# The forget row moved into the low keys' free rows: two score products a step in the second block's attention

## What is computed

```python
def forgetting_attention(q, k, v, log_f):
    """q, k, v: (B, H, S, Dh); log_f: (B, H, S) float32 log forget gates."""
    c = jnp.cumsum(log_f, axis=-1)
    qf = q.astype(jnp.float32) * (Dh ** -0.5)
    for i in range(S // Q_BLOCK):
        q0, q1 = i * Q_BLOCK, (i + 1) * Q_BLOCK
        logits = jnp.einsum('bhqd,bhkd->bhqk', qf[:, :, q0:q1], kf[:, :, :q1])
        logits = logits + c[:, :, q0:q1, None] - c[:, :, None, :q1]
        logits = jnp.where(s_pos <= t_pos, logits, -jnp.inf)
        p = jax.nn.softmax(logits, axis=-1)
        outs.append(jnp.einsum('bhqk,bhkd->bhqd', p, vf[:, :, :q1]))
```

## Time and profile of the kernel before

| | us |
|---|---|
| three runs | 1095.19, 1095.08, 1096.62 |
| median | 1095.19 |
| the profiled execution, its own time | 1095.96 |
| its span in the profile | 1094.1 |
| around the span | 1.9 |
| mean granted clock of TensorE, share of full speed | 0.997 |
| busy TensorE matmuls, share of the span | 97% |
| busy VectorE | 81% |
| busy ScalarE | 61% |
| busy GpSimd | 17% |

### The profile page before, as it was taken

The page is one execution under the profiler, slowest core; times in us unless marked ns, Lnnn a source line. Parts: engine busy times, 40 slices in busy tenths (PEclk is TensorE's granted clock), DMA queues, the critical chain, the costliest instruction groups (busy, mean ns, idle before and its releaser), DMA issues.

```text
span 1094.1 us, 18024 instructions
## 1 busy us (share of the span) xinstructions
PE 1065.5 (97%) x6544; PEld 939.3 (86%) x6544; DVE 885.8 (81%) x1448; ACT 666.9 (61%) x1179; POOL 186.2 (17%) x239
## 2 busy tenths in 40 slices
PE   8999988999999999999999998999999999999997
PEld 6688876998999999888888777778899999998885
DVE  6888885798988888888684778666689889879876
ACT  7787785476555555656683477545445555566664
POOL 1486744011001111000000103300001111100000
PEclk9999999999999999999999999999999999999999
DMA  7423321766765676886536721045356676776553
GB/s 285 114 77 81 92 60 38 243 126 191 202 158 190 175 189 209 194 246 205 190 126 214 180 58 39 21 110 179 96 136 183 205 176 181 203 183 214 189 177 123
DMA packets 51320, 171.17 MB, mean 156 GB/s; under 512 B 6432, under 2 KB 7072, under 8 KB 51104
## 3 DMA queue, kind: packets, MB, share of 16 engines
q1 hardware_dynamic: 37296, 122.56, 34.3%
q0 software_dynamic: 13312, 46.14, 19.4%
q10 hardware_dynamic: 624, 1.31, 0.4%
HBM read 162.64 MB, written 48.23 MB: 193 GB/s over the span
## 4 chain that ended last, share of the span: by engine, by line
PE 84%; DVE 7%; ACT 5%; issue 2%; POOL 1%; DMA 1%; ACTq 0%; SPq 0%; DVEq 0%; POOLq 0%
PE bank L2090 11%; PE bank L2092 11%; PE bank L2091 11%; PE bank L2651 6%; PE bank L2653 6%; PE bank L2652 6%; PE bank L583 6%; PE bank L584 6%; PE bank L585 6%; PE bank L1148 2%; PE bank L1138 2%; PE bank L1093 1%; PE bank L1094 1%; PE bank L1095 1%; DVE wl L506 1%
## 5 line engine op out<-in xcount | busy, mean ns | idle before, releaser
L506 DVE TENSOR_TENSOR wl<-raw,wh 128x1024 fp32r<-128x1024 f32 (+1 forms) x144 | 169.6, 1184 | 63.1 <-ACT wh L493 61.5
L493 ACT ACTIVATE wh<-raw 128x1024 fp32r<-128x1024 f32 (+1 forms) x145 | 145.7, 1010 | 114.1 <-PE bank L2653 52.9
L2090 PE MATMUL bank<-h,wh 128*128 128x256 f32 x576 | 163.2, 283 | 2.2 <-DVE sw L2270 2.2
L2092 PE MATMUL bank<-h,wl 128*128 128x256 f32 x576 | 163.0, 283 | 0.0
L2091 PE MATMUL bank<-h,wh 128*128 128x256 f32 x576 | 163.0, 283 | 0.0
L2091 PE MATMUL bank<-hl,wh 128*128 128x256 f32 x432 | 122.3, 283 | 0.0
L2092 PE MATMUL bank<-hh,wl 128*128 128x256 f32 x432 | 122.2, 283 | 0.0
L2090 PE MATMUL bank<-hh,wh 128*128 128x256 f32 x432 | 122.2, 283 | 0.0
L2651 PE MATMUL bank<-wh,high_tokens 128*128 128x512 f32 x308 | 121.2, 394 | 0.7 <-DVE wl L506 0.7
L2653 PE MATMUL bank<-wh,low_tokens 128*128 128x512 f32 x308 | 120.0, 390 | 0.0
L2652 PE MATMUL bank<-wl,high_tokens 128*128 128x512 f32 x308 | 120.0, 390 | 0.0
(11 more groups left out here) (337 smaller groups left out, 2660.8 us busy)
## 6 DMA issues: line engine op xcount, KB each, us to landing
raw<-weights SPq DMA_DIRECT2D x163, 512.0 KB, 4.2
down_weight_sums<-weights POOLq DMA_DIRECT2D x60, 512.0 KB, 6.0
raw<-down_weight_sums SPq DMA_DIRECT2D x40, 512.0 KB, 4.0
down_weight_sums<-down_weight_sums POOLq DMA_DIRECT2D x20, 512.0 KB, 4.7
xres<-x_t SPq DMA_DIRECT2D x8, 512.0 KB, 6.7
down_weight_sums<-weights POOLq DMA_DIRECT2D x12, 256.0 KB, 4.1
sw<-ta SPq DMA_DIRECT2D x36, 64.0 KB, 2.0
raw<-down_weight_sums SPq DMA_DIRECT2D x8, 256.0 KB, 2.6
```

Source lines behind the costliest of these rows:

```text
L493: act.activation(wh[:, j, b, n], raw[:, j, b, n], ACT.Copy).then_inc(high_split, 1)
L506: v.tensor_tensor(wl[:, j, b, :], raw[:, j, b, :], wh[:, j, b, :].bitcast(F32), ALU.subtract)\
L2090: pe.matmul(o, wh_half[:, h, k, :], high[:, k, :], start=first and k == 0, stop=False, skip_group_check=True)
L2092: ins = pe.matmul(o, wl_half[:, h, k, :], high[:, k, :], start=False, stop=k == HK - 1, skip_group_check=True)
```

## The change

The forget row gets no product of its own. Its row for one head (high and low part) is put in the `other` rows of the low keys: `act_forget_rows` multiplies the 64 first rows of `cs` by the one-hot column of the head, on ScalarE, in iterations 12 to 15 of the in-projections, and `act_other_keys` goes. The second score product then takes another stationary operand, `q2[par]`: a copy of the queries' high part in `own`, ones in `other`. So it gives high queries times low keys, plus the forget row. The product of low queries with low keys is no longer computed.

`q2` has two query slots per `par`. Its ones come from one DMA per `par` on ScalarE's queue in iteration 14, its queries from one DMA per head on ScalarE's queue: the first two in iteration 16, the other six in attention steps 2, 6, 10, 14, 18 and 22, one step after the late query's high part is made. TensorE waits for the copy before a head's first score (`query_placed`).

To make room, `pr2` holds only the key blocks that are used (`ROW2`, 20 KB instead of 32 KB), and six of the eight buffers of turned probabilities move behind it; `q2` takes the place of `tb` and `sw`.

```diff
+ROW2 = [j * (j + 1) // 2 * P for j in range(QB + 1)]
...
-        pr2 = place("pr2", [P, PR2, QB, S], at=hh_at)
+        pr2 = place("pr2", [P, PR2, ROW2[QB]], at=hh_at)
...
+        pth2 = [place(f"pth2_{i}", [P, S], F32R, at=hh_at + (20 + 2 * i) * KB if i < 3 else arena + 70 * KB) for i in range(PT2)]
+        ptl2 = [place(f"ptl2_{i}", [P, S], F32R, at=hh_at + (26 + 2 * i) * KB if i < 3 else rh_at + 2 * KB) for i in range(PT2)]
+
+        q2 = [place(f"q2_{par}", [P, 2, S], F32R, at=at) for par, at in ((0, tb_at), (1, tb_at + 4 * KB))]
...
-                    if f + ph.lag[f] + 1 == m and ph.tiles[f][1] == "k":
-                        act_other_keys(act, ph, f)
+                if 12 <= m < 16:
+                    act_forget_rows(act, ph, m - 12)
+                if m == 14:
+                    act_ones_rows(act, ph)
+                if m == 16:
+                    q0 = tile_of(ph, "q", 0)
+                    act.wait_ge(ph.fin.high, ph.fin_count(q0))
+                    for par in range(2):
+                        act_place_query(act, 0, par)
...
+        def act_forget_rows(act, ph, g):
+
+            act.wait_ge(ph.fin.low, ph.low_count(IN2.index(("forget", "c", 0))))
             for par, own, other in pair():
-                ins = act.activation(ph.kl[par][other, i, :], ph.kl[par][own, i, :].bitcast(F32), ACT.Copy)
+                head = 2 * g + par
+                ins = act.activation(ph.kl[par][other, g, :], cs[0:HD, :].bitcast(F32), ACT.Copy, scale=col("onehot", head, slice(0, HD)))
             ins.then_inc(ph.keys, 1)
+
+        PLACED1 = 32 * len(PLACED)
+
+        def act_ones_rows(act, ph):
+
+            act.wait_ge(ph.fin.low, ph.low_count(ph.pools[-1]))
+            for par, own, other in pair():
+                act.dma_start(q2[par][other, :, :].rearrange("p r (b n) -> p (r b) n", n=P).bitcast(F32),
+                              ones[other, :].rearrange("p (b n) -> p b n", b=1).to_broadcast([HD, 2 * QB, P])).then_inc(f1.placed[par], 16)
+
+        def act_place_query(act, qt, par):
+
+            own = list(pair())[par][1]
+            act.wait_ge(f1.placed[par], PLACED1 + 16 * (qt + 1))
+            act.dma_start(q2[par][own, qt % 2, :].bitcast(F32), stacked[par][own, qt, :].bitcast(F32)).then_inc(f1.placed[par], 16)
+
+        def query_placed(eng, qt, par):
+
+            eng.wait_ge(f1.placed[par], PLACED1 + 16 * (qt + 2))
...
+                query_placed(pe, qt, par)
...
-            pe.matmul(o, q, in2.kl[par][:, kt, keys], start=False, stop=False)
-            pe.matmul(o, onehot[:, aux:aux + 1].to_broadcast([P, P]), cs[:, keys], start=False, stop=False)
+            pe.matmul(o, q2[par][:, qt % 2, block], in2.kl[par][:, kt, keys], start=False, stop=False)
...
+                for m, par in WAITING_HIGH:
+                    if n == WAITING_HIGH[m, par] + 1:
+                        act.wait_ge(late.high, late_count(m, par))
+                        act_place_query(act, in2.tiles[m][2], par)
```

More of the change, by code:

```diff
@@ L415, in build @@
         tq = place("tq", [P, 3, S], at=arena + 64 * KB)
-        pth2 = [place(f"pth2_{i}", [P, S], F32R, at=turn_at + 2 * i * KB if i < 3 else arena + 70 * KB) for i in range(PT2)]
-        ptl2 = [place(f"ptl2_{i}", [P, S], F32R, at=turn_at + (6 + 2 * i) * KB if i < 3 else rh_at + 2 * KB) for i in range(PT2)]
+        pth2 = [place(f"pth2_{i}", [P, S], F32R, at=hh_at + (20 + 2 * i) * KB if i < 3 else arena + 70 * KB) for i in range(PT2)]
+        ptl2 = [place(f"ptl2_{i}", [P, S], F32R, at=hh_at + (26 + 2 * i) * KB if i < 3 else rh_at + 2 * KB) for i in range(PT2)]
+        q2 = [place(f"q2_{par}", [P, 2, S], F32R, at=at) for par, at in ((0, tb_at), (1, tb_at + 4 * KB))]
         v2 = place("v2", [P, QB, 2, 4 * P], F32R, at=arena + 72 * KB)
@@ L1873, in pe_turn2 @@
             for q in range(q0, q1_):
-                ins = pe.transpose(turn_bank2(n)[:, q * P:(q + 1) * P], pr2[:, s % PR2, q, kb * P:(kb + 1) * P], ident[:, :])
+                ins = pe.transpose(turn_bank2(n)[:, q * P:(q + 1) * P], pr2[:, s % PR2, ROW2[q] + kb * P:ROW2[q] + (kb + 1) * P], ident[:, :])
             ins.then_inc(at2.turned, 1)
@@ L1906, in vec_attention2 @@
                         v.wait_ge(at2.turned, 4 * (s - PR2) + 4)
-                    v.tensor_scalar(pr2[:, s % PR2, j, lo * P:hi * P], banks[n % 3][:, lo * P:hi * P], -SCALE, None,
+                    v.tensor_scalar(pr2[:, s % PR2, ROW2[j]:ROW2[j + 1]], banks[n % 3][:, lo * P:hi * P], -SCALE, None,
                                     ALU.mult, ALU.min, accum_out=negm[:, n % 8:n % 8 + 1]).then_inc(at2.maxed, 1)
@@ L1948, in act_attention2 @@
                     act.wait_ge(at2.maxed, n + 1)
-                    p = pr2[:, s % PR2, j, lo * P:hi * P]
+                    p = pr2[:, s % PR2, ROW2[j]:ROW2[j + 1]]
                     act.activation(p, p, ACT.Exp, bias=negm[:, c], scale=-1.0, accum_out=rsum[:, c]).then_inc(at2.exped, 1)
+                for m, par in WAITING_HIGH:
+                    if n == WAITING_HIGH[m, par] + 1:
+                        act.wait_ge(late.high, late_count(m, par))
+                        act_place_query(act, in2.tiles[m][2], par)
                 for m, par in WAITING_HIGH:
@@ L1963, in gpsimd_attention2 @@
             for n in range(at2.n):
-                lo, hi = key_range("causal", n % 4)
-                p = pr2[:, (n // 4) % PR2, n % 4, lo * P:hi * P]
+                p = pr2[:, (n // 4) % PR2, ROW2[n % 4]:ROW2[n % 4 + 1]]
                 g.wait_ge(at2.inverted, n // 2 + 1)
```

3 lines of the change are left out of this document (removed).

## The result

| | before | after |
|---|---|---|
| median of 20 runs each, us | 1095.30 | 1097.49 |
| lowest to highest | 1094.76 to 1096.69 | 1095.57 to 1099.46 |
| ratio to before, 95% interval | | 1.0016 [1.0010, 1.0023] |
| the profiled execution / its span | 1095.96 / 1094.1 | 1096.74 / 1094.9 |
| granted clock of the profiled execution | 0.997 | 0.994 |

The changed kernel is slower by 0.16%. Its interval keeps this difference from zero, though it lies under the 0.2% that the prediction held for invisible. The forecast was 1096.0; 1.5 us are missing from it.

The account below looks back on a forecast made before the run. The prediction took a VectorE-ScalarE loop in the second block's attention as the bound, TensorE outside. Terms +0.8 - 0.2 + 0.2 = +0.8 us on a median of 1095.19 gave 1096.0 us, range 1092.5 to 1099.0.

Parts of the forecast that it names:

- Bound of the stage: Second block's attention, 657.0 to 697.6 us: VectorE and ScalarE form the loop, 6.09 us a head, with TensorE outside.
- Rival 1: TensorE's queue bounds the attention after all, so all 5.2 us saved there come: 1090.8 us, chance 0.12.
- The heads' pitch: First maxima of neighbouring heads in the attention stay about 6.1 us apart; falling towards 5.5 us would mean Rival 1.
- TensorE's idle time in the stage: Sign in the changed trace: TensorE's idle time in the attention goes up by about 5 us.
- Place of the forget rows: On ScalarE before the attention, all four pairs now stand behind 642 us, delaying the first maximum: +0.8 us, bounds -0.2 to +1.3.
- the splits of the output projection: On ScalarE they begin at 656.1 us instead of 654.96; VectorE starts its half at 657.2 instead of 656.40.
- scaled form: Forget rows as scaled copies on ScalarE: scale priced at nothing, bound 0.03 us each, 0.3 us in all.
- Product: Forget product removed from each score step; on the path only once, at the attention's start: 0.2 us gained, 0 to 0.6.
- Six issues: Six query-copy DMA issues on ScalarE's queue in the attention, 0.73 us each against 0.70 hidden: +0.2 us, bounds 0 to 4.4.
- Ones rows: Two DMA issues filling ones on ScalarE's queue before the attention, between third pair and split: +0 us, bound +1.5.
- First query copy: Issued by about 657.1 us at the latest, landing in 2.3 us before VectorE is ready: cost 0, bound +0.5 or more.
- The forecast end of the stage: Sign in the changed trace: the second block's attention ends at about 698.4 us, 697.6 before.

Follow-up runs that it names:

- e1: The kernel before without the forget product, so the forget row is left out of the scores: 1095.99 us, ratio 1.0000.
- e9: The kernel before without the forget product, with seven extra 128x512 matmuls on TensorE just ahead of the first score: 1095.12 us, ratio 0.9997.
- e7: The kernel before, all three products, with its eight low-key copies made by GpSimd in place of ScalarE: 1094.73 us, ratio 0.9987.
- e6: The changed kernel with the eight forget rows made by GpSimd in place of ScalarE: 1093.76 us, ratio 0.9983.
- e8: e6 with late high parts of query tiles 1 and 2 and query head 1's copies moved before the attention on ScalarE: 1093.50 us, ratio 0.9977.
- e10: The changed kernel with three extra 128x512 matmuls on TensorE ahead of its wait for the first query copy: 1096.77 us, ratio 1.0011.
- e2: The kernel before with its four pairs of key copies moved to iterations 12 to 15, where the changed kernel has forget rows: 1097.04 us, ratio 1.0011.
- e3: The changed kernel with seven extra 512-column matmuls on TensorE ahead of its wait for the first query copy: 1097.41 us, ratio 1.0017.
- e5: The changed kernel with each of the six query copies inside the attention issued as two DMAs of 32 partitions: 1099.83 us, ratio 1.0037.
- e4: The changed kernel, heads 0 and 1 using 64-row second products and a separate forget product, without waiting for query copies: 1101.33 us, ratio 1.0051.

## Why the prediction came out as it did

- **Bound of the stage** (loop of VectorE and ScalarE, TensorE outside): right. Without the product the time doesn't move (e1, e9); work taken off ScalarE moves the end of the stage by 1.25 (e7), 1.94 (e6) and 3.3 us (e8). Rival 1 is refuted. The heads' pitch stayed at 6.1 us as forecast. TensorE's idle time in the stage rose from 5.5 to 8.4 us, not by about 5, since at the low clock its matmuls take longer; in e10, which kept the clock, it was 9.3 us even with the three added ones counted as work.
- **Place of the forget rows, +0.8**: right, 0.87. The steps landed too: the splits of the output projection began 14.1 us behind the anchor (656.1 - 642.09 = 14.0 predicted), VectorE's half 15.2 us (15.1 predicted). But it was put together otherwise: 0.61 for the place (e2) and 0.26 for the scaled form, priced at 0 with a bound of 0.3.
- **Product, -0.2**: right in size, -0.24 to -0.25, only where the clock is kept (e3, e9, e10).
- **Six issues, +0.2**: 0. Each takes 0.47 us, not 0.73: the median of the earlier trace rows was of other copies. The mechanism was the right one (e5). In the sum this 0.2 too much and the product's 0.2 cancel, so the forecast of +0.8 is the place alone.
- **Ones rows, 0**: right. Issues of 0.73 and 0.65 us at 648.25 and 649.01, beside key copies already pushed.
- **First query copy, 0**: right for the path, wrong for the copy. It was issued at 654.35, beside the fourth pair, where the prediction had 657.1 at the latest, and took 3.8 us to land in place of 2.3; one error made good for the other, which was luck. The first scores came at 658.31, and it was said that behind TensorE's wait "stand only scores". True, but TensorE stood idle, and the term that failed is the one that isn't in the sum: **the fall of the granted clock to 0.50 at the stage's start, +0.63 us** in the trace. The prediction took the clock of 1.00 in the earlier trace rows as given. The change takes work from TensorE just where it is already waiting: 1.39 us before, 2.07 us and shorter scores after.

The sum with what was measured: +0.87 - 0.25 + 0 + 0.63 = +1.25, against 1.26 in the traces. The medians are 2.2 us apart, and the ratio's interval goes from 1.1 to 2.5 us: the trace of one execution lies inside it near its lower end. The rest of that difference isn't settled. The forecast end of the stage, 698.4, stands in the trace (698.42) by luck: the anchor came 0.49 us early, and the stage was 0.5 us longer than forecast.

**Left open.** The DMA wait and the lost product each make TensorE's work at the start thinner. That the lost product alone suffices is shown (e1 against e9). Whether the wait alone would do it in a kernel that keeps the product wasn't tried; e2, which keeps it and starts late, has the lower mean clock in 6 of 11 executions, and no trace says where it fell. What makes the clock fall in one execution and not in the next is open as well. And e3's median.

## What to carry to other kernels

Taking work from an engine that isn't the bound isn't free of risk: where TensorE already waits, a shorter stretch of work can halve its clock, and then it is on the path. Read the granted clock in the windows around the place, before and after, compare it with the mean clock of the other executions, and try a few matmuls there whose results nobody reads. A step that moves costs by its place: look for the engine that is idle between its inputs and its use (here GpSimd, 1.9 us in e6), before looking for a cheaper form.

## What the runs showed of the hardware

- TensorE's clock fell to 0.50 for over six microseconds behind an idle time of 2.07 us (after) and of 1.80 us (e1), and in e4 behind two of 0.39 and 0.59 us; e2's trace kept it at 1.00 with 1.60 us. Three matmuls of 512 columns in the gap kept it at 1.00 in e10's trace. Near 149 us it fell in eight of twelve traces, with the same idle times of 0.6 to 1.0 us in traces with and without the fall.
- A DMA issue on ScalarE's queue of 0.47 us beside an exponential of 0.70 with read-out costs nothing; two cost 0 to 0.56 us by place.
- A product with 64 rows between ones of 128 takes longer to start and to follow: 0.39 and 0.40 us at a clock of 0.50 with 128 columns, against 0.22 to 0.25.
- The ones' fill, 256 KB, took 3.5 to 3.8 us to land; a query copy of 128 KB mostly 2.2 to 2.5 us, the first one 3.8 us, beside the weight loads (DMA share 0.68 from 654 to 657 us).
- Beside GpSimd's products VectorE's SBUF operations slow down: two of `kl` 1.78 us against 1.40, the split 1.60 against 1.23; behind GpSimd's last one two splits take 2.36 us again, as before. The Trainium skill ("Perfetto Trace Analysis", Optimizing Scalar/DVE Operations) says that the two share a read port of SBUF, so that moving work between them might not help. The slower rows agree with the sharing; but the work came from ScalarE, and here it did help.
